# A two-layer diffusion backbone on one core: the first turned queries and keys move beside the last unit of the Fourier merge, and in layer 1 the first merges go between the rotated tiles

## The reference

```python
def _merge(gz, oa, ob, oc, w_branch, w_out):
    ga, gb, gf = jnp.split(jax.nn.sigmoid(gz), N_BRANCH, axis=-1)
    y = ga * (oa @ w_branch[0]) + gb * (ob @ w_branch[1]) + gf * (oc @ w_branch[2])
    return y @ w_out

def _token_mixers(h, hc, w_in, q_norm, k_norm, rpb, w_branch, w_out, rows, cols, rows_n, with_ctx_out):
    ...
    qa, ka, va, qb, kb, vb, uc, gz = jnp.split(h @ w_in, IN_SPLITS, axis=-1)
    qa = _rope_2d(_rmsnorm(qa.reshape(B, L, A_HEADS, HEAD_DIM), q_norm), rows, cols)
    ka = _rope_2d(_rmsnorm(ka.reshape(B, L, A_KV_HEADS, HEAD_DIM), k_norm), rows, cols)
    ...
    k_all = jnp.concatenate([kac, ka], axis=1)
    v_all = jnp.concatenate([vac, va], axis=1)
    ...
    oa = lax.map(lambda qq: _gqa(qq, k_all, v_all), q_blocks)
    ...
    oc = _fourier_mix(uc)

    y = _merge(gz, oa, ob, oc, w_branch, w_out)
```

## Time and profile before

| | us |
|---|---|
| median of 3 runs | 2425.41 (2423.21 to 2426.27) |
| the profiled execution's own time | 2428.46 |
| its span, first to last instruction | 2426.2 |
| layer 0: `merge_c`, then the start of attention A | 157 to 257.6, then to 274 |
| layer 1: `merge_c`, then the start of attention A | 1513 to 1587.7, then to 1602 |

### The profile page before, as it was taken

The page is one execution under the profiler, slowest core; times in us unless marked ns, Lnnn a source line. Parts: engine busy times, 40 slices in busy tenths (PEclk is TensorE's granted clock), DMA queues, the critical chain, the costliest instruction groups (busy, mean ns, idle before and its releaser), DMA issues.

```text
span 2426.2 us, 34451 instructions
## 1 busy us (share of the span) xinstructions
PE 2292.5 (94%) x13082; PEld 2093.1 (86%) x13082; DVE 1195.2 (49%) x2401; ACT 947.6 (39%) x1850; POOL 1090.1 (45%) x844
## 2 busy tenths in 40 slices
PE   8999899998899999999999989899988899999997
PEld 4899888987799999999999878778877789888887
DVE  6979666435542355653821263556535525212124
ACT  4232566335532651111121254266435537422223
POOL 1434455334433554433533443446434457644545
PEclk9999999999999999999999999999999999999999
DMA  6624100211113545443421542211212246422335
GB/s 256 236 93 147 62 27 27 64 63 51 54 56 112 169 139 200 138 145 115 161 82 61 165 142 88 78 44 36 77 58 73 62 148 193 146 95 95 113 114 181
DMA packets 118798, 264.90 MB, mean 109 GB/s; under 512 B 13444, under 2 KB 13700, under 8 KB 117256
## 3 DMA queue, kind: packets, MB, share of 16 engines
q1 hardware_dynamic: 109728, 238.08, 29.6%
q10 hardware_dynamic: 8936, 25.04, 3.1%
HBM read 252.58 MB, written 10.49 MB: 108 GB/s over the span
## 4 chain that ended last, share of the span: by engine, by line
PE 78%; DVE 12%; ACT 4%; issue 2%; DMA 1%; POOL 1%; ACTq 0%; SPq 0%; DVEq 0%
PE ps L1843 29%; PE ps L1845 13%; PE ps L1855 13%; PE ps L1956 6%; PE ps L2220 6%; PE ps L2184 4%; PE ps L2165 2%; DVE pt_lo L1588 2%; PE ps L2134 1%; PE ps L2030 1%; DVE max_c L1571 1%; DVE ps L1563 1%; DVE ada_unused_gate_up L1144 1%; DVE max_c L1560 1%; POOL p_sb L568 1%
## 5 line engine op out<-in xcount | busy, mean ns | idle before, releaser
L556 POOL TENSOR_TENSOR w_lo<-raw,w_hi 128x512 fp32r<-128x512 f32 x632 | 866.3, 1394 | 970.7 <-ACT w_hi L630 970.3
L630 ACT ACTIVATE w_hi<-raw 128x512 fp32r<-128x512 f32 x632 | 367.0, 627 | 686.4 <-PE ps L1845 246.2
L568 POOL TENSOR_TENSOR p_sb<-p_sb,row_inv 128x768 f32<-128x768 f32 (+2 forms) x160 | 185.5, 1170 | 302.3 <-DVE row_inv L1581 301.7
L1843 PE MATMUL ps<-h_hi,w_lo 128*128 128x384 f32 (+1 forms) x832 | 300.6, 361 | 0.0
L1843 PE MATMUL ps<-h_lo,w_hi 128*128 128x384 f32 (+1 forms) x832 | 300.4, 361 | 0.0
L1843 PE MATMUL ps<-h_hi,w_hi 128*128 128x384 f32 (+1 forms) x832 | 300.4, 361 | 0.0
L1671 DVE TENSOR_TENSOR ps<-silu_g,ps 128x768 f32<-128x768 f32 (+3 forms) x52 | 37.8, 726 | 376.7 <-PE ps L1845 177.9
L1843 PEld LDWEIGHTS ps<-h_hi,w_hi 128*128 128x128 f32 x832 | 156.2, 188 | 16.0
L1843 PEld LDWEIGHTS ps<-h_lo,w_hi 128*128 128x128 f32 x832 | 156.2, 188 | 15.9
L1843 PEld LDWEIGHTS ps<-h_hi,w_lo 128*128 128x128 f32 x832 | 156.2, 188 | 15.8
L2220 PE MATMUL ps<-h_hi,w_lo 128*128 128x384 f32 (+1 forms) x408 | 136.8, 371 | 27.2 <-DVE k_ll L1528 14.9
(11 more groups left out here) (248 smaller groups left out, 5491.5 us busy)
## 6 DMA issues: line engine op xcount, KB each, us to landing
raw<-in_stream SPq DMA_DIRECT2D x632, 256.0 KB, 2.8
ada_raw_gate_up<-in_w_ada SPq DMA_DIRECT2D x48, 512.0 KB, 3.5
bias_sb<-in_bias ACTq DMA_DIRECT2D x32, 320.0 KB, 2.8
ada_raw_tokens_a<-in_w_ada SPq DMA_DIRECT2D x16, 512.0 KB, 3.6
ada_raw_merge_c<-in_w_ada SPq DMA_DIRECT2D x16, 512.0 KB, 3.5
scratch<-xr ACTq DMA_DIRECT2D x16, 512.0 KB, 4.2
xr<-scratch SPq DMA_DIRECT2D x14, 512.0 KB, 4.7
first_raw<-in_w_first SPq DMA_DIRECT2D x5, 1024.0 KB, 14.1
```

What stands on the lines that cost most here:

```text
L556: nc.gpsimd.tensor_tensor(w_lo[:, u % 2, cols], raw[:, u % 2, cols], w_hi[:, u % 2, cols].bitcast(F32), ALU.subtract).then_inc(S("lo_made" ...
L568: nc.gpsimd.tensor_tensor(p, p, row_inv[:, c:c + 1].broadcast_to([P, keys]), ALU.mult).then_inc(S("p_ready"), 1)
L630: nc.scalar.activation(w_hi[:, s, cols], raw[:, s, cols], ACT.Copy).then_inc(S("hi_made"), 1)
L1843: last = nc.tensor.matmul(bank(0), tile, x[:, k, 0:split], start=start, stop=stop)
```

## The change

It does four things.

- The start pieces move from the head of `attention` into the last unit of `merge_c`, on all three engines. On TensorE the first two stand ahead of unit 11's first branch product and the others between its two products. They go to banks 0 to 3, one each, instead of banks 4 and 5 by turns (`turn_bank`).
- VectorE's share of the pieces stands ahead of the last two merges, and ScalarE's ahead of its wait for unit 11. In layer 0 ScalarE first waits for the last modulation unit, whose buffers the keys overwrite. A new count after unit 11's first product (`branch_half`) lets VectorE merge that half early.
- `attention` now begins on TensorE with the first scores; the first fills come behind them. ScalarE loads the exponential's table after the pieces and the last split, and then waits for the last merge.
- In layer 1, VectorE rotates tiles 0 and 1, does the first two merges, and rotates tiles 2 to 5 (`ROTATED_FIRST`). The loops of `merge_c` on TensorE and ScalarE are written out.

```diff
+ROTATED_FIRST = (ALLT, 2)
```

ScalarE, the merge and the head of attention:

```diff
             def merge_c(ph):
-                with act.Fori(0, 2) as i:
...
+                nxt = after(ph)
+                for n in range(12):
+                    c = 2 * (n // 3) + n % 3
...
+                    if n == 11:
+                        if not ph.layer:
+                            act.wait_ge(S("ada_used"), PRIME - ADA_FIRST + ADA_WINDOWS[ph.kind][1])
+                        for name in start_pieces(nxt):
+                            piece(nxt, *name)
+                    unit_done(ph.unit + n, n % 2, use if n % 3 < 2 else None)
...
                 load_table(ACT.Exp)
-                start = start_pieces(ph)
-                for name in start:
-                    piece(*name)
+                act.wait_ge(S("merged"), at(ph, "merged"))
                 probs(0, 0)
```

VectorE, the end of `fourier` and the merge:

```diff
-                rotate(ph)
+                rotate(ph, 0, ROTATED_FIRST[ph.layer])
...
                 for c in range(KD):
-                    pair(acc[:, c, 0:w], c, 3 * (c // 2) + 3)
+                    if c == KD - 2:
+                        for name in start_pieces(after(ph)):
+                            piece(after(ph), *name)
+                    pair(acc[:, c, 0:w], c)
                     if c % 2 and not ph.layer:
                         ada_units(ph.kind, n, n + ADA_AFTER_PAIR[c // 2])
                         n += ADA_AFTER_PAIR[c // 2]
+                    if c == 1 and ROTATED_FIRST[ph.layer] < ALLT:
+                        rotate(ph, ROTATED_FIRST[ph.layer], ALLT)
```

TensorE, the branch unit of the merge, the head of attention, and the banks:

```diff
             def merge_c(ph):
...
+                    pe.wait_ge(S("o_lo"), at(ph, "o_lo"))
+                    if n == 11:
+                        pe.wait_ge(S("rope_step"), at(nxt, "rope_step"))
+                        pe.wait_ge(S("gated"), at(ph, "gated") + KD - 1)
+                        for name in start_pieces(nxt)[:2]:
+                            piece(nxt, *name)
+                    for c in range(2):
+
+                        pe.wait_ge(S("merged"), at(ph, "merged") + pair + c - 1)
+                        last = columns(ph, u, n % 2, fixed(4 + 2 * c, ph.width > LAT), oc_hi, oc_lo, KB, first=KB * c)
+                        if n == 11 and c == 0:
+                            last.then_inc(S("branch_half"), 1)
+                            pe.wait_ge(S("gated"), at(ph, "gated") + KD)
+                            for name in start_pieces(nxt)[2:]:
+                                piece(nxt, *name)
+                    last.then_inc(S("unit_done"), 1)
...
                 if branch == 0:
-                    start = start_pieces(ph)
-
-                    pe.wait_ge(S("merged"), at(ph, "merged"))
-                    pe.wait_ge(S("rope_step"), at(ph, "rope_step"))
-                    for name in start[:2]:
-                        piece(*name)
-                    fill(-2, 0)
-                    for name in start[2:]:
-                        piece(*name)
-                    fill(-2, 1)
+                    pe.wait_ge(S("lo_out"), at(ph, "lo_out") + len(start_pieces(ph)))
                     score(0, 0)
                     score(0, 1)
+                    pe.wait_ge(S("merged"), at(ph, "merged"))
+                    fill(-2, 0)
+                    fill(-2, 1)
...
+def turn_bank(ph, order):
+
+    return order if order < len(start_pieces(ph)) else TURN_BANK[ph.part] + order % 2
```

More of the change, by code:

```diff
@@ L914, in turned_hi @@
                     act.wait_ge(S("turned_p"), at(ph, "turned_p") + order + 1)
[L915 to L929, removed]
+                    nc.scalar.activation(pt_hi[branch][:, a:a + w], ps[:, turn_bank(ph, order), 0:w], ACT.Copy).then_inc(S("hi_out"), 1)
                 def move_half(n):
@@ L1399, in tokens_a, with piece @@
                                         v_a[:, :, :, 0:HD].bitcast(F32), ALU.subtract).then_inc(S("va_lo"), 1)
-            def rotate(ph):
-                step = chain("rope_step", at(ph, "rope_step") - ROTATE_STEPS)
-                invs = inv_s[:, :].rearrange("p (t h) -> p t h", t=ALLT)
[L1405 to L1411, removed]
+            def piece(ph, what, h, part):
+                order = turn_order(ph)[what, h, part]
+                a, b = ((0, LAT), (LAT, TOK))[part]
+                dve.wait_ge(S("hi_out"), at(ph, "hi_out") + order + 1)
+                for x in range(2):
+                    rows, other = slice(HD * x, HD * x + HD), slice(HD * (1 - x), HD * (2 - x))
+                    if what == "q":
+                        src, dst, hi = rows, q_st[0][h][x][other, a:b], q_st[0][h][x][rows, a:b]
+                    else:
+                        src = slice(HD * h, HD * h + HD)
+                        dst, hi = k_ll[0][rows, h, a:b], k_hh[0][src, h, a:b]
+                    last = nc.vector.tensor_tensor(dst, ps[src, turn_bank(ph, order), 0:b - a], hi.bitcast(F32), ALU.subtract)
+                last.then_inc(S("lo_out"), 1)
@@ L1587, in turned_lo @@
                     dve.wait_ge(S("hi_out"), at(ph, "hi_out") + order + 1)
[L1588 removed]
+                    nc.vector.tensor_tensor(pt_lo[branch][:, a:a + w], ps[:, turn_bank(ph, order), 0:w], pt_hi[branch][:, a:a + w].bitcast(F32),
                                             ALU.subtract).then_inc(S("lo_out"), 1)
[L1591 to L1598, removed]
[L1599 to L1604 removed]
                 def fold(n):
@@ L1629, in attention @@
                 for name in slot_pieces(ph, -1):
-                    piece(*name)
+                    piece(ph, *name)
                 invert(0, 0)
@@ L2137, in score @@
                     last.then_inc(S("scored"), 1)
-                def piece(what, h, part):
-                    order = turns[what, h, part]
-                    a, b = ((0, LT), (LT, ALLT))[part]
-                    if order > 1:
-                        pe.wait_ge(S("lo_out"), at(ph, "lo_out") + order - 1)
-                    for t in range(a, b):
-                        col = P * h if what == "q" else P * KB
-                        src = tok_a[:, t, col:col + P]
-                        last = nc.tensor.transpose(ps[:, TURN_BANK[branch] + order % 2, (t - a) * P:(t - a + 1) * P], src, ident[:, :])
-                    last.then_inc(S("turned_p"), 1)
                 def turn(n, g):
```

98 lines of the change are left out of this document (56 added, 42 removed).

## The result

The changed kernel takes 2406.51 us (median of four runs, 2405.64 to 2407.31) against 2425.84 for the kernel before: ratio 0.9922, 95% interval 0.9905 to 0.994. That is 19.3 us less (by the interval, 14.6 to 23.0); the forecast was 2406.4, or 19.0 less.

What follows compares the result with a forecast made beforehand. TensorE, busy 2292.5 of 2426.2 us, bounds the kernel, so time is won only where it waits or runs slowly. 7.28 + 5.33 + 6.4 = 19.0 us off 2425.41 gives 2406.4; range 2402 to 2415 (0.85).

Steps and rivals of the forecast that it cites:

- Layer 1, the merge: Unit 4's end to unit 11's: wait and slow clock go, ten transposes cost 1.36; 7.28 us less.
- The 6.80 and the 1.84: Layer 1: TensorE's 6.80 us wait before unit 5 and 1.84 us for the lower clock behind it; both go.
- Unit 8: Layer 1: its merge of chunks 2 and 3 becomes the next late one, but 8.7 us of cover make it free.
- Layer 1, the start: Unit 11's end to first turned probabilities: 8.54 us of scores and fills without a gap instead of 13.87; 5.33 less.
- Layer 0: Merge and attention start: first turned probabilities at 267.5 instead of 273.94 us; 6.4 less.
- The copy's wait: Layer 0: a fill still waits 0.67 us for ScalarE's copy of its first half.
- The cover of 0.4: Layer 0: VectorE's last piece ends at 257.9 us, 0.4 before TensorE wants it.
- Loops, tables, `branch_half`: Written-out loops, second sigmoid table load and the new count: cost nothing, bounds 0 and some tenths of a us per layer.
- Attention gives the start back: Rival: attention's VectorE-set pace loses the earlier start, only the merge's gain stays; 2418.1 us, chance 0.10.
- The modulation: Rival, layer 0: ScalarE's wait for the modulation replaces the removed wait, layer 0 wins nothing; 2412.8 us, chance 0.09.
- The clock: Rival: short waits left in layer 0 bring one more slow clock stretch, priced 1.84 us; 2408.2 us, chance 0.06.

Runs made afterwards that it cites:

- e2: The kernel before with only layer 1's rotation divided after tile 1 for the first two merges; 2417.85 us, ratio 0.9967 to the kernel before.
- e1: The changed kernel with layer 1's rotation in one piece ahead of the merges again; 2417.08 us, ratio 0.9966 to the kernel before.
- e4: The kernel before with the merge's loops written out on TensorE and ScalarE, nothing moved; 2427.02 us, ratio 1.0008 to the kernel before.
- e5: The changed kernel with layer 0's start pieces and first fills back at their old places; 2414.12 us, ratio 0.9952 to the kernel before.
- e6: The changed kernel, but layer 0's ScalarE pieces wait for the first half of unit 11; 2408.76 us, ratio 0.9926 to the kernel before.
- e7: The changed kernel, but layer 0's ScalarE pieces wait for all of unit 11; 2413.36 us, ratio 0.9947 to the kernel before.
- e8: The changed kernel with five rotated tiles instead of two ahead of layer 1's first merges; 2415.75 us, ratio 0.996 to the kernel before.
- e9: The changed kernel with layer 0's second-pair scores before the last eight fills, second exponential before the gate copy; 2407.45 us, ratio 0.9927.
- e10: The changed kernel with four rotated tiles instead of two ahead of layer 1's first merges; 2411.04 us, ratio 0.9939 to the kernel before.
- e3: The changed kernel with the first fills ahead of the first scores again; 2411.94 us, ratio 0.9944 to the kernel before.

## Why the prediction was right, step by step

The mechanism was right in all three parts: the waits that were to go are gone, and only one of 0.26 us came in their place. That the sum is off by only 0.3 us is in part luck. The first two terms were too small by 0.20 and 0.33 and the third too large by 0.25, and a jump of 1.3 us in layer 0, for which the forecast had no term, did not fall into the profiled execution.

- **Layer 1, the merge: -7.28 forecast.** Unit 4's end to unit 11's is 1572.88 - 1533.64 = 39.24 instead of 46.72: -7.48. Unit 11 with its ten transposes takes 1572.88 - 1566.28 = 6.60, against 5.44 without: 1.16, where I took 1.36 because I counted the overlap of their end. The 6.80 and the 1.84 are both gone; e2 and e1 show that they go together with the divided rotation alone. Unit 8 did not wait.
- **Layer 1, the start: -5.33 forecast.** Unit 11's end to the turn is 8.21 instead of 13.87: -5.66. As forecast, nothing stands there but TensorE's own scores and fills. GpSimd's normalising began at 1576.70 and took 2.89, so the probabilities were ready at 1579.59, 1.5 early (1.7 forecast).
- **Layer 0: -6.4 forecast, -6.15 measured.** Unit 11 began 0.14 later, counted from the merge's start. The forecast 0.16 agrees by chance: the eight transposes fit wholly into the wait, 0.18 of it is left, and so they cost nothing. The 0.14 is the weights' own arrival, 92.84 us after the merge's start, against 92.61 to 93.04 in the four kernels without transposes there (before, e2, e4, e5). The copy's wait is 0.67 as forecast. A wait of 0.26 for the last merges came in addition: unit 11 ended 0.35 earlier than forecast, VectorE's merges on time. The cover of 0.4 was 0.09 in the trace; e6 and e7 show what its lack costs.
- **Loops, tables, `branch_half`: 0 forecast.** e4 shows it for the loops; no wait of TensorE or ScalarE names the others.
- **The rivals.** *Attention gives the start back*: from the first turn to the end of VectorE's last `o_sum` it took 430.32 - 273.94 = 156.38 in layer 0 before and 425.32 - 269.53 = 155.79 after, in layer 1 1718.17 - 1601.62 = 116.55 and 1697.59 - 1581.09 = 116.50. Nothing was given back. *The modulation* released the pieces as feared, but the transposes beside unit 11 left it just enough time. *The clock* did not fall: behind 0.26 and 0.67 it stayed at 1.00.
- **The jump in layer 0**: unit 11 begins 92.83 to 92.99 us after the merge's start in five kernels (after, e1, e8, e9, e10) and 94.07 to 94.20 in three (e3, e6, e7), with the same work of TensorE ahead of it. GpSimd's `w_lo`, for which it waits, starts 0.10 to 0.31 ahead of one of VectorE's modulation instructions in the five and 0.07 to 0.52 behind one in the three; the rows are in the last section. The cause is read from the traces; no run set this order by an edit. In an execution of the second kind the changed kernel would have won about 4.9 us in layer 0 instead of 6.15 (an estimate: 6.15 less the 1.23 by which e3's unit 11 is later).
- **Still open**: what shifts the two starts against each other by some tenths. ScalarE's split ahead of `w_lo` waits for the weights' transfer; no run tells what moves it or VectorE's chain.

By the Trainium skill, "TensorE: Matmul & The Clock Gate", Part 1, the clock follows how busy TensorE has recently been. The rows agree: 0.50 behind waits of 5.32, 5.70, 6.57 and 6.80, 1.00 behind 1.09 and 2.07. The length of a single wait is not all: in layer 0 before, three short waits close together brought the clock to 0.55.

```profile
259.47 1.09 PE L2148 MATMUL ps<-ident,tok_a 128*128 128x128 f32 x8 [1.91 <-DVE acc L1466]
...
262.90 0.44 PE L2148 MATMUL ps<-ident,tok_a 128*128 128x128 f32 x2 [0.92 <-DVE k_ll L1603]
264.20 0.56 PE L2148 MATMUL ps<-ident,tok_a 128*128 128x128 f32 x2 [0.86 <-DVE q_st L1603]
```

The price on top of a single long wait was 1.35 to 2.68, so my single 1.84 was one value out of a spread.

## What to carry to other kernels

A long job on a helper engine that stands ahead of a short one can cost the main engine twice, by its wait and by the slow clock behind it; look for the short job's inputs being ready long before, and split the long job there. The start of a phase can be prepared beside the last unit of the phase before when free banks are at hand, but each engine of its chain needs cover: here TensorE's transposes cost 1.16 us in layer 1, and 0.1 us of slack was left on VectorE in layer 0. Where runs spread by several us, read a part worth a few us from a stretch between two named instructions, and check that what lies ahead of the edit in that stretch has not moved.

## What the runs showed of the hardware

The same modulation instruction (128x1024, two inputs in SBUF) took VectorE 1.22 us alone and 2.1 to 2.2 beside GpSimd's `w_lo`; GpSimd took 6.99 for four of those beside it and 2.53 for two later on. Which of the two starts first decides which one loses. In the changed kernel `w_lo` starts 0.25 ahead of a modulation instruction. The first of the four `w_lo` then takes 1.28, and the last two modulation instructions take 2.11 and 2.18:

```profile
249.41 6.99 POOL L557 TENSOR_TENSOR w_lo<-raw,w_hi 128x512 fp32r<-128x512 f32 x4 [11.37 <-ACT w_hi L631]
...
249.66 2.11 DVE L1147 SCALAR_TENSOR_TENSOR ada_unused_merge_c<-ada_raw_merge_c,ada_cond_merge_c 128x1024 bf16<-128x1024 f32 x1
...
251.81 2.18 DVE L1147 SCALAR_TENSOR_TENSOR ada_unused_merge_c<-ada_raw_merge_c,ada_cond_merge_c 128x1024 bf16<-128x1024 f32 x1
```

In e7 `w_lo` starts 0.34 behind one. That one takes its 1.23, the first `w_lo` takes 2.02, and only the last modulation instruction is longer:

```profile
248.12 1.23 DVE L1148 SCALAR_TENSOR_TENSOR ada_unused_merge_c<-ada_raw_merge_c,ada_cond_merge_c 128x1024 bf16<-128x1024 f32 x1
...
248.46 6.74 POOL L557 TENSOR_TENSOR w_lo<-raw,w_hi 128x512 fp32r<-128x512 f32 x4 [11.96 <-ACT w_hi L631]
...
249.39 2.17 DVE L1148 SCALAR_TENSOR_TENSOR ada_unused_merge_c<-ada_raw_merge_c,ada_cond_merge_c 128x1024 bf16<-128x1024 f32 x1
```

In e3 and e6 it is as in e7: `w_lo` starts 0.07 and 0.52 behind, and its first instruction takes 2.28 and 1.84. In all three, unit 11 starts 1.27 after that modulation instruction has ended. In the changed kernel it starts 1.43 after `w_lo` has begun (250.84 - 249.41). So where `w_lo` came second, nearly all of its work was done after the other's end, that is, it stood still until then.

This is the jump of 1.3 us in layer 0. It has a second side: where `w_lo` comes second, VectorE loses once and not twice, and the modulation ends 95.0 to 95.2 after the merge's start instead of 96.0. VectorE's last piece, which ends 0.09 before unit 11's last product in the changed kernel's trace, ends 1.7 before it in e3. So late weights shorten VectorE's chain and lengthen TensorE's: layer 0 has two limits close to each other.

The Trainium skill, "SBUF — State Buffer", section "Who interferes with whom", says that a VectorE instruction with two SBUF inputs contends with a GpSimd instruction that reads SBUF, that the ports they share are an exclusive lock, and that the order of issue decides who blocks. The rows of both kinds agree: 1.28 and 2.11 where `w_lo` was first, 1.23 and 2.02 where the modulation was.
